# Adding the skip term of an SSD output on VectorE instead of through an identity product on TensorE

## What is computed

```python
y_f, h_f = ssd_scan(xs, dt[:, :, 0], a[0], bs, cs, h0[0])
y_b, h_b = ssd_scan(flip(xs), flip(dt[:, :, 1]), a[1], flip(bs), flip(cs), h0[1])
y = y_f + flip(y_b) + d_skip[:, None] * xs
```

## Time and profile before

| what | us |
|---|---|
| median of 3 runs | 3648.97 (3638.85 to 3649.78) |
| the profiled execution | 3642.95 |
| its span, first to last instruction | 3641.0 |

### The profile page before, as it was taken

One profiled execution on the slowest core, in us unless ns is written; L12 is line 12 of the kernel. 1 busy time (PEld: TensorE's weight loads), 2 busy tenths in 40 slices (PEclk: granted clock), 3 DMA queues, 4 the chain that ended last, 5 costly groups with the idle time before them and its releaser, 6 DMA issues. The chain is left out here.

```text
span 3641.0 us, 37882 instructions
## 1 busy us (share of the span) xinstructions
PE 3271.6 (90%) x14980; PEld 2567.9 (71%) x14980; DVE 1653.4 (45%) x1893; ACT 962.5 (26%) x1788; POOL 333.1 (9%) x220
## 2 busy tenths in 40 slices
PE   7899999998999699957999979999985999993776
PEld 7688888876887467746888858888773555552565
DVE  2744543573034067764444344233244555543444
ACT  2422221111211155422222231332221434334000
POOL 0100000000012045530000000000000000000111
PEclk9999999999999778878999989999996999996888
DMA  4212323332245335543333242232223212202111
GB/s 158 83 57 62 112 76 126 138 116 75 106 138 199 116 115 158 157 139 114 112 115 121 87 155 82 94 104 70 81 64 89 53 30 59 76 7 81 72 72 69
DMA packets 210679, 358.39 MB, mean 98 GB/s; under 512 B 21780, under 2 KB 143252, under 8 KB 202657
## 3 DMA queue, kind: packets, MB, share of 16 engines
q1 hardware_dynamic: 198550, 333.91, 28.4%
q10 hardware_dynamic: 4608, 16.78, 1.3%
q0 software_dynamic: 7392, 5.89, 0.8%
HBM read 234.64 MB, written 121.74 MB: 98 GB/s over the span
## 5 line engine op out<-in xcount | busy, mean ns | idle before, releaser
L634 PE MATMUL p_ps<-hmT_hi,p_w_hi 128*128 128x512 f32 x1312 | 524.6, 400 | 21.5 <-ACT p_work L355 15.9
L634 PE MATMUL p_ps<-hmT_hi,p_w_lo 128*128 128x512 f32 x1312 | 513.9, 392 | 0.0
L634 PE MATMUL p_ps<-hmT_lo,p_w_hi 128*128 128x512 f32 x1312 | 513.3, 391 | 0.0
L1727 PE MATMUL p_ps<-h2T_hi,p_w_hi 128*128 128x512 f32 x800 | 327.3, 409 | 19.3 <-DVE h2T_lo L1589 19.3
L1727 PE MATMUL p_ps<-h2T_hi,p_w_lo 128*128 128x512 f32 x800 | 314.5, 393 | 0.0
L1727 PE MATMUL p_ps<-h2T_lo,p_w_hi 128*128 128x512 f32 x800 | 314.2, 393 | 0.0
L634 PEld LDWEIGHTS p_ps<-hmT_hi,p_w_hi 128*128 128x128 f32 x1312 | 248.0, 189 | 75.6 <-issue 21.2
L634 PEld LDWEIGHTS p_ps<-hmT_hi,p_w_lo 128*128 128x128 f32 x1312 | 248.0, 189 | 53.1
L634 PEld LDWEIGHTS p_ps<-hmT_lo,p_w_hi 128*128 128x128 f32 x1312 | 248.3, 189 | 49.5
L1866 PE MATMUL t_psO<-t_prob,t_v 128*65 128x512 f32 (+3 forms) x640 | 261.6, 531 | 1.0
L1921 ACT ACTIVATE t_prob<-t_psS 128x1024 f32<-128x1024 f32 (+1 forms) x160 | 150.1, 938 | 320.5 <-PE t_psS L1854 184.9
(11 more groups left out here) (356 smaller groups left out, 5904.5 us busy)
## 6 DMA issues: line engine op xcount, KB each, us to landing
p_w_raw<-in_w_in SPq DMA_DIRECT2D x66, 512.0 KB, 5.9
p_spare<-in_wada ACTq DMA_DIRECT2D x32, 512.0 KB, 5.5
p_spare<-scratch_xs_tok SPq DMA_DIRECT2D x19, 512.0 KB, 4.5
scratch_xs_tok<-p_work SPq DMA_DIRECT2D x8, 1152.0 KB, 6.1
p_work<-in_wada SPq DMA_DIRECT2D x16, 512.0 KB, 3.6
p_work<-in_x SPq DMA_DIRECT2D x16, 512.0 KB, 3.5
scratch_dT<-p_work SPq DMA_DIRECT2D x8, 1024.0 KB, 5.9
scratch_zpT<-p_work SPq DMA_DIRECT2D x8, 1024.0 KB, 4.0
```

What stands on the lines that cost most here:

```text
L634: mm = pe.matmul(PS[:, c, 0:width], wt[n][:, q, :], xx[:, q, cols], start=(q == 0 and j == 0), stop=(q == KT - 1 and j == 2))
L1727: mm = pe.matmul(ps[:, c, :], wt[n][:, q, :], xx[:, q, c * CH:(c + 1) * CH], start=(q == 0 and j == 0), stop=(q == KT - 1 and j == 2))
```

## The change

The skip term is no longer a product. PE's two products L996 in each turn are gone, `inside` starts psY itself, and VectorE adds `y_xskip` in a pass of its own at the end of `backward`, behind which `summed_y` is signalled now. Since VectorE reads `y_xskip` there, POOL's next `skip` waits for `summed_y` of the turn before and no longer for `inside`. PE waits for `y_xs` and no longer for `skip`; SP waits for both before it loads a new `y_xs`.

```diff
@@ SP
                         sp.wait_ge(S["inside"], c + 1)
+                        sp.wait_ge(S["skip"], c + 1)
                         load_xs(c + 2)
@@ POOL, skip(c)
                     if c >= 1:
-                        g.wait_ge(S["inside"], c)
+                        g.wait_ge(S["summed_y"], c)
                     g.tensor_tensor(by_head(xk[:]), by_head(xs[c % 2][:]), heads_of(dskip[:]), ALU.mult).then_inc(S["skip"], 1)
@@ DVE, backward(c)
-                    v.tensor_tensor(y[c % 2][:], y[c % 2][:], tmp[:], ALU.add).then_inc(S["summed_y"], 1)
+                    step(v.tensor_tensor(y[c % 2][:], y[c % 2][:], tmp[:], ALU.add))
+                    v.wait_ge(S["skip"], c + 1)
+                    v.tensor_tensor(y[c % 2][:], y[c % 2][:], xk[:], ALU.add).then_inc(S["summed_y"], 1)
@@ PE
-                def skipped(q):
-                    pe.matmul(psY[:, q * CH:(q + 1) * CH], s.ident[:], xk[:, q * CH:(q + 1) * CH],
-                              start=True, stop=False, skip_group_check=True)
                 def inside(c, heads):
...
-                                       start=False, stop=h % 8 == 7, skip_group_check=True)
+                                       start=True, stop=True, skip_group_check=True)
...
-                    pe.wait_ge(S["skip"], c + 1)
+                    pe.wait_ge(x_in[c % 2], 16 * (c // 2 + 1))
                     if c >= 1:
                         pe.wait_ge(S["forward"], c)
-                    skipped(0)
                     inside(c, range(0, 4))
...
-                    skipped(1)
```

## The result

| kernel | median us (runs) | ratio to before, 95% interval |
|---|---|---|
| before | 3648.97 (5) | 1 |
| changed | 3763.81 (5) | 1.0319 (1.0304 to 1.0334) |

The change makes the kernel 3.2% slower: 115 us between the medians, and 120.9 us between the spans of the two profiled executions (3641.0 and 3761.9 us). The forecast was 3772 us.

The account below looks back on a forecast made before the run. PE was taken to bound the loop; late rows and a halved clock make 13 turns 29.9 instead of 20.5 us, +122 us, and the last turns +1: 3643 + 123 = 3766 us, median 3772 us, range 3690 to 3803 us.

Parts of the forecast that it names:

- PE bounds the loop, and the moved wait decides: In the 13-turn loop PE is busy 266.67 of 266.7 us; POOL's skip, waiting for the new pass, delays the rows.
- Three passes, 3.78 us: VectorE after the backward read's start: three passes of 1.26 us each, 3.78 us, before POOL's skip can start.
- The skip, 2.98 us behind them: POOL's skip, held by VectorE's next pass, ends 2.98 us behind the third pass; 1.91 us if not held.
- The issues, 1.13 us: Row transfers queued on POOL behind the skip: 1.13 us from its end until the second y_seg_l transfer is issued.
- The landing, 2.5 us: Row transfers from issue to arrival: 2.5 us in the median, 2.1 to 7.2 us, closing a chain of 10.4 us.
- PE's wait, 3.6 to 5.3 us: PE waits for late rows before its exponents, 3.6 to 5.3 us in each of turns 1 to 13.
- The clock: After PE's wait the mixed stretch and backward offset run at 1.2 GHz: a turn 29.9 us, without that 21.3 us.
- Turn 0 and the end: Turn 0, without late rows: between -2 and +2 us, taken as 0; turns 14 and 15: +1 us.
- The 6 us added from execution to median: Whole kernel: the median of runs lies 6 us above the profiled execution, so 3766 us becomes 3772 us.
- the price of the products: PE's two identity products: 1.81 us a turn at full clock, 29 us over 16 turns, if PE sets the time.
- rival (c): Rows are not late in the loop; PE's 29 us come off, 3620 us, taken as 3628 us; chance 0.07.
- Rival (b): PE's wait is there but the clock stays up, needing waits nearer 3.15 than 3.97 us: 3659 us; chance 0.08.

Follow-up runs that it names:

- moved_wait: Kernel before, with one thing of the change: POOL's skip also waits for summed_y; products kept, no new pass. 3766.37 us, ratio 1.0335.
- rows_first: Changed kernel, but POOL issues the row transfers ahead of the skip. 3646.74 us, ratio 1.0002.
- filled_spread: Changed kernel, PE's wait filled by four needless forward offsets a turn, heads and exponents evenly mixed, sums in the stretch. 3680.88 us, ratio 1.0089.
- before_spread: Kernel before, heads and exponents evenly mixed, sums one by one in the stretch, skip products ahead of heads 0 and 8. 3658.47 us, ratio 1.0027.
- no_products: Kernel before, with the two identity products left out and nothing in their place. 3648.06 us, ratio 1.0005.
- even_two: Changed kernel with two skip buffers, the offset's and sums' products spread behind the exponent pairs, L958 moved into VectorE's idle time. 3683.92 us, ratio 1.0094.

## Why the prediction was right, point by point

- **PE bounds the loop, and the moved wait decides**: right. The moved wait alone gives 1.0335 (moved_wait), its removal 1.0002 (rows_first).
- **Three passes, 3.78 us**: 1440.39 - 1436.61 = 3.78 us. **The skip, 2.98 us behind them**: it ends at 1443.38 us, 2.99 us. **The issues, 1.13 us**: the second of L847 begins at 1443.91 + 0.60 = 1444.51 us, 1.13 us.
- **The landing, 2.5 us**: the term that was a little small. From 1444.51 to PE's start at 1447.49 us it is 2.98 us, the step to PE included; the chain is 10.9 us, not 10.4 us.
- **PE's wait, 3.6 to 5.3 us**: 5.2 us on the mean, 5.7 us at most.
- **The clock**: right. It fell during the wait, stayed at 0.50 for the whole stretch (15.9 us, as forecast) and rose in or behind the backward offset, listed with 3.45 us at 1463.40 us (forecast 3.6 us). The turn is 30.2 us for 29.9 us. That the clock is a cause was only argued then; filled_spread shows it. That it doesn't come back within such a stretch holds for the changed kernel, but not everywhere: in before_spread, with denser products in the stretch, it did.
- **Turn 0 and the end**: 0 and +1 us forecast, +2.9 us and 0 us measured within the stage (the clock fell in turn 0's stretch at 1306 us; 2.9 us is beyond the +2 us that I allowed).
- **How close the total is owes something to luck**: the 13 turns cost 125.5 us for the 122 us forecast, and turn 0 cost 2.9 us where none was forecast, but -7.6 us of spread in other stages took that back. The 6 us added from execution to median had no counterpart: the changed kernel's profiled execution is its median.
- **Wrong: the price of the products**, in the part on what the change takes away and in rival (c). I took 1.81 us a turn at full clock as 29 us that would come off if the rows were in time, and put the rival at 3628 us. rows_first and no_products put it at 3647 and 3648 us: the clock takes it all back. The step that failed is reading a cost from full-clock rows while the clock's mean, 0.86, depends on the very work that is removed. I had even written that turn 0 might lose its gain by a longer unbroken stretch, and did not carry that over to the other turns.
- Rival (b)'s threshold was too kind: I read from the last stage that a wait of 3.15 us leaves the clock alone. Here waits of 0.9 and 1.9 us (moved_wait) or 2.4 us (even_two), with sparse products around them, went with a fall. A length of a wait read in one stage doesn't hold in another.

## What to carry to other kernels

Before moving a wait, list everything that is queued behind it on that engine: here three small transfers behind a GpSimd pass cost 3%, though the pass itself was not urgent; issue such transfers first. On TensorE, a dense product between sparse ones may pay for itself through the clock: read the granted clock with and without it before counting it as overhead, and try spreading it before removing it. Keeping some dense work in one block may help as well: in the changed kernel a fallen clock came back in such a block. But that is a guess from traces, not tested by itself.

## What the runs showed of the hardware that I had not expected

- The clock fell to 1.2 GHz with PE busy without a gap: in no_products the 13 turns have 273.40 us of busy PE in 273.40 us at a mean of 0.74. The Trainium skill (TensorE: Matmul & The Clock Gate, section HAM oscillation) ties the fall to gaps in which PE waits; the changed kernel, with waits of 5.2 us, agrees with it. In no_products there is no such gap, and the measurement decides. The kernel before showed it already, with 0.86 in a loop that is busy throughout.
- More work on PE made the kernel faster: filled_spread, with 6.9 us of needless products a turn, by 83 us against the changed kernel.
- A pass of GpSimd that started 0.11 us behind a VectorE pass with two SBUF inputs took 2.88 us in place of 1.91 us, while VectorE's, the one that had begun, took its usual 1.22 us.
